# A one-core layer with 32 experts: order of the routing weights, of the second expert's copies, of two experts' loads and of the last squares

## The reference, cut to what matters

```python
lg = (t @ p['w_router_group'] + p['b_router_group']).astype(F32)
pg = jax.nn.softmax(lg, axis=-1)
grp = jnp.argmax(lg, axis=-1)
...
top_p, top_i = lax.top_k(pe, TOP_K)
wts = p_grp * top_p / jnp.sum(top_p, axis=-1, keepdims=True)
...
for e in range(N_EXPERTS):
    z = jax.nn.silu(t @ p['w1'][e]) * (t @ p['w3'][e])
    y = y + gates[:, e:e + 1] * (z @ p['w2'][e])
...
x = x + g2 * hier_moe(h, p)
y_sample = rmsnorm(xs, g_final)
```

## Time and profile before

| | |
|---|---|
| median of 3 runs | 979.88 us (977.21 to 982.35) |
| profiled execution | 981.13 us |
| its span, first to last instruction | 979.3 us |
| busy, PE / DVE / POOL / ACT | 91% / 61% / 32% / 28% of the span |
| chain of work that ended last, by engine | PE 59%, DMA 19%, DVE 15%, ACT 4% |
| granted clock of PE, mean | 0.974 |

### The profile page before, as it was taken

One profiled execution on the slowest core, in us unless ns is written; L12 is line 12 of the kernel. 1 busy time (PEld: TensorE's weight loads), 2 busy tenths in 40 slices (PEclk: granted clock), 3 DMA queues, 4 the chain that ended last, 5 costly groups with the idle time before them and its releaser, 6 DMA issues.

```text
span 979.3 us, 12372 instructions
## 1 busy us (share of the span) xinstructions
PE 890.1 (91%) x4480; PEld 552.6 (56%) x4480; DVE 594.1 (61%) x957; ACT 278.0 (28%) x468; POOL 310.2 (32%) x232
## 2 busy tenths in 40 slices
PE   3898898999899999999899999999989888889994
PEld 1688796989899999845333333333333333333331
DVE  2589696859211552235447677677767666657667
ACT  4374636463143432011211111112111111212112
POOL 0046262636255545222222133133222131313100
PEclk9799899999999999999789999999999999999998
DMA  9962272646464347445689999999999999999981
GB/s 343 358 226 94 78 254 97 224 142 237 172 215 165 137 152 262 177 205 212 252 309 417 407 415 424 415 419 413 396 392 414 398 404 394 410 400 410 408 355 66
DMA packets 59849, 285.69 MB, mean 292 GB/s; under 512 B 6655, under 2 KB 11039, under 8 KB 47252
## 3 DMA queue, kind: packets, MB, share of 16 engines
q1 hardware_dynamic: 56196, 278.63, 73.5%
q0 software_dynamic: 2480, 3.11, 1.1%
q10 hardware_dynamic: 1120, 3.24, 0.9%
HBM read 286.80 MB, written 3.19 MB: 296 GB/s over the span
## 4 chain that ended last, share of the span: by engine, by line
PE 59%; DMA 19%; DVE 15%; ACT 4%; issue 2%; SPq 1%; DVEq 0%; POOL 0%; ACTq 0%
PE bank L1084 12%; PE bank L1097 8%; PE bank L878 7%; PE bank L879 7%; PE bank L880 7%; DMA ring<-in_w 7%; DMA slot<-in_w 6%; PE bank L934 4%; PE bank L1085 4%; DMA gate_w<-in_w 3%; DVE xcy L1672 3%; DVE xcy L2038 3%; DMA ring<-in_w_ada 2%; PE bank L1061 2%; PE bank L814 1%
## 5 line engine op out<-in xcount | busy, mean ns | idle before, releaser
L475 POOL TENSOR_TENSOR subs<-ring,subs 128x1024 fp32r<-128x1024 f32 x69 | 177.6, 2581 | 222.2 <-ACT subs L1225 222.2
L878 PE MATMUL bank<-h_hl,subs 128*128 128x384 f32 x488 | 167.8, 344 | 12.0 <-ACT lru L1304 4.6
L879 PE MATMUL bank<-h_hl,subs 128*128 128x384 f32 x488 | 165.7, 340 | 0.0
L880 PE MATMUL bank<-h_hl,subs 128*128 128x384 f32 x488 | 165.6, 339 | 0.0
L2013 DVE TENSOR_TENSOR lru<-bank,cp 128x512 f32<-128x512 f32 x186 | 116.3, 678 | 55.0 <-PE bank L1061 55.0
L1084 PE MATMUL bank<-ring,x_T 128*64 128x512 f32 x256 | 119.6, 611 | 8.2 <-DMA ring<-in_w 3.3
L1085 PE MATMUL bank<-ring,x_T 128*64 128x512 f32 x256 | 118.1, 604 | 0.0
L2022 DVE TENSOR_TENSOR hg<-hg,lru 128x512 f32<-128x512 f32 x186 | 116.6, 679 | 0.0
L878 PEld LDWEIGHTS bank<-h_hl,subs 128*128 128x128 f32 x488 | 92.9, 190 | 19.3 <-issue 9.6
L665 POOL COPY idx<-lists 64x1 uint32 (+1 forms) x31 | 5.5, 177 | 294.8 <-PE bank L1039 294.8
L1084 PE MATMUL bank<-slot,x_T 128*64 128x512 f32 x192 | 88.6, 605 | 8.5 <-DMA slot<-in_w 6.0
(11 more groups left out here) (245 smaller groups left out, 1506.0 us busy)
## 6 DMA issues: line engine op xcount, KB each, us to landing
ring<-in_w SPq DMA_DIRECT2D x46, 2048.0 KB, 26.6
slot<-in_w SPq DMA_DIRECT2D x36, 2048.0 KB, 27.1
ring<-in_w_in SPq DMA_DIRECT2D x14, 2048.0 KB, 8.0
ring<-in_w_ada SPq DMA_DIRECT2D x12, 2048.0 KB, 9.1
gate_w<-in_w SPq DMA_DIRECT2D x12, 2048.0 KB, 26.9
ring<-in_w_rnn_out SPq DMA_DIRECT2D x2, 2048.0 KB, 8.4
ring<-in_w_conv_out SPq DMA_DIRECT2D x2, 2048.0 KB, 8.1
ring<-in_w_o SPq DMA_DIRECT2D x2, 2048.0 KB, 8.2
```

The lines of the kernel that those rows point to most:

```text
L475: eng.tensor_tensor(pair[:, 1], src, pair[:, 0].bitcast(F32), ALU.subtract).then_inc(done, 1)
L878: eng.matmul(ps[:, 0:T], pair[:, 1, k, :], x[:, 0, k, :], start=(k == 0), stop=False)
L879: eng.matmul(ps[:, 0:T], pair[:, 0, k, :], x[:, 1, k, :], start=False, stop=False)
L880: mm = eng.matmul(ps[:, 0:T], pair[:, 0, k, :], x[:, 0, k, :], start=False, stop=(k == KD - 1))
```

## The change

Four places are written in another order.

1. DVE works out the three tiles' weights ahead of the copies of the list, and ACT takes the exponentials ahead of the copies of expert 0's rows. POOL copies expert 0's weight column directly behind its token column, ahead of the gather for expert 1; the waits for the stored rows move behind it.
2. For expert 0, ACT and DVE copy the transposed rows of expert 1 ahead of the parts of y.
3. Expert 30 is loaded in the pieces in which expert 31 is: its w1 now waits for y of expert 27 too. Its `hidden` waits in two steps.
4. At the end ACT squares tile t + 1 ahead of the root of tile t.

```diff
@@ -400,5 +400,5 @@
         gated = sem("spread_times_gain")
         added = sem("spread_added")
-        half_landed = [sem(f"last_half_landed{w}") for w in range(2)]
+        half_landed = [[sem(f"half_landed{x}{w}") for w in range(2)] for x in range(2)]
         last_y_ready = sem("last_y_times_gain")
         step_v = sem("vector_step")
@@ -615,17 +615,23 @@
                 for s in range(LAP):
                     load_expert(i * LAP + s, s)
-            for s in range(LAP - 1):
+            for s in range(LAP - 2):
                 load_expert(NE - LAP + s, s)
-            multiplied_in(NE - 4)
-            multiplied_out(NE - 4)
-            part = KD * CW // 2
-            for w, src in enumerate((w1_v, w3_v)):
-                eng.dma_start(moe_slots[moe_slot(LAP - 1, w)][:, 0:part], src[NE - 1][:, 0:part])\
-                    .then_inc(half_landed[w], 16)
-            for w, src in enumerate((w1_v, w3_v)):
-                n = moe_slot(LAP - 1, w)
-                eng.dma_start(moe_slots[n][:, part:], src[NE - 1][:, part:]).then_inc(moe_landed[n], 16)
-            multiplied_in(NE - 3)
-            load(NE - 1, LAP - 1, 2)
+
+            def load_in_halves(e, s):
+
+                part = KD * CW // 2
+                multiplied_in(e - 3)
+                multiplied_out(e - 3)
+                for w, src in enumerate((w1_v, w3_v)):
+                    eng.dma_start(moe_slots[moe_slot(s, w)][:, 0:part], src[e][:, 0:part])\
+                        .then_inc(half_landed[LAP - 1 - s][w], 16)
+                for w, src in enumerate((w1_v, w3_v)):
+                    n = moe_slot(s, w)
+                    eng.dma_start(moe_slots[n][:, part:], src[e][:, part:]).then_inc(moe_landed[n], 16)
+                multiplied_in(e - 2)
+                load(e, s, 2)
+
+            for s in (LAP - 2, LAP - 1):
+                load_in_halves(NE - LAP + s, s)
             eng.wait_ge(flag_ready, 1)
             most = eng.value_load(flag[0:1, 0:1], min_val=0, max_val=T)
@@ -734,13 +740,13 @@
             wait_read(eng, ("list",))
             eng.wait_ge(flag_ready, 1)
+            token_column(0, 0)
+            eng.wait_ge(slot_weights, 1)
+            weight_column(0, 0)
             for t in range(TT):
                 eng.wait_ge(h2_out[t], 16)
-            token_column(0, 0)
             eng.wait_ge(xg_used, 1)
             gather(1, 1)
             token_column(1, 1)
-            eng.wait_ge(slot_weights, 1)
-            for e in range(2):
-                weight_column(e, e)
+            weight_column(1, 1)
             for e in range(2, 4):
                 eng.wait_ge(xg_used, e - 1)
@@ -1068,7 +1074,8 @@
                 if not first:
                     eng.wait_ge(z_ready, e)
-                if last:
-                    eng.wait_ge(half_landed[0], 16)
-                    eng.wait_ge(half_landed[1], 16)
+                halves = isinstance(i, int) and i == NE // LAP - 1 and s >= LAP - 2
+                if halves:
+                    eng.wait_ge(half_landed[LAP - 1 - s][0], 16)
+                    eng.wait_ge(half_landed[LAP - 1 - s][1], 16)
                 else:
                     wait_weights(eng, i, s, 0)
@@ -1079,5 +1086,5 @@
                     if k == 3:
                         between()
-                    if last and k == KD // 2:
+                    if halves and k == KD // 2:
                         wait_weights(eng, i, s, 0)
                         wait_weights(eng, i, s, 1)
@@ -1480,4 +1487,6 @@
             root(2)
             store(2)
+            for t in range(TT):
+                top_exps(t)
             ps, _ = tile(("x0",))
             eng.wait_ge(h2_out[1], 16)
@@ -1486,6 +1495,4 @@
             eng.activation(x_T[:, 0:4, :], bank[FIRST_T[0]][:, :].rearrange("p (m t) -> p m t", m=4)[:, :, 0:HALF], ACT.Copy)\
                 .then_inc(xT_a, 1)
-            for t in range(TT):
-                top_exps(t)

             def rows_copy(e):
@@ -1519,8 +1526,8 @@
                     rows_copy(e + 1)
                 zT_copy(e)
+                if first:
+                    rows_copy(1)
                 if not last:
                     y_hi(i, s, e)
-                if first:
-                    rows_copy(1)

             for s in range(LAP):
@@ -1554,4 +1561,10 @@
                 eng.wait_ge(o_added, TT)

+            def last_root(t):
+
+                eng.wait_ge(mean_ready, TT + t + 2)
+                eng.activation(stat[:, 2, 2, t:t + 1], stat[:, 2, 1, t:t + 1], ACT.Sqrt)\
+                    .then_inc(rms_ready, 1)
+
             eng.activation(stat[:, 1, 2, 0:1], stat[:, 1, 1, 0:1], ACT.Sqrt)
             for t in range(TT):
@@ -1561,7 +1574,7 @@
                 eng.activation(o_junk, x_rows[:, t, :], ACT.Square, accum_out=stat[:, 2, 0, t:t + 1])\
                     .then_inc(ssq_ready, 1)
-                eng.wait_ge(mean_ready, TT + t + 2)
-                eng.activation(stat[:, 2, 2, t:t + 1], stat[:, 2, 1, t:t + 1], ACT.Sqrt)\
-                    .then_inc(rms_ready, 1)
+                if t:
+                    last_root(t - 1)
+            last_root(TT - 1)
             eng.wait_ge(state_out, 16)

@@ -1978,4 +1991,6 @@
             wait_read(eng, ("count",))
             eng.tensor_copy(flag[:, :], cmax[:, :]).then_inc(flag_ready, 1)
+            for t in range(TT):
+                weights(t)
             ps, free = tile(("list",))
             eng.tensor_scalar(slot_token[:, :], ps[:, 0:NE], float(UNUSED), None, ALU.add)
@@ -2061,6 +2076,4 @@
                                                   in1=last_gain[rows, :], op0=ALU.mult, op1=ALU.add))

-            for t in range(TT):
-                weights(t)
             eng.wait_ge(weights_done, 1)
             eng.tensor_copy(slot_weight[:, :], bank[7][0:CAP, 0:NE]).then_inc(slot_weights, 1)
```

## The result

The changed kernel takes 981.96 us (median of 20 runs, 978.56 to 984.02) where the kernel before, run beside it, takes 978.73 (20 runs). The ratio is 1.0024, with an interval of 1.0015 to 1.0032: slower by some 2 to 3 us. The forecast was 2.25 us faster. The change lies within 0.5%, yet its sign was wrong, and a version with one of its parts taken back (the first experiment) is 0.45% faster than the kernel before. The profiled execution of after took 983.96 us (span 982.1).

What follows compares the result with a forecast made beforehand. The weight stream bounds the middle; only its restart at expert 1, the stall before expert 30 and the tail can move the end. 0 + 0.65 - 1.8 - 1.1 = -2.25 us gave a median of 977.6 us, range 975.0 to 981.8.

Steps and rivals of the forecast that it cites:

- What bounds the kernel: Middle of the expert stage: lasts as long as its weight transfers; the stream restarts when expert 1's hidden products finish.
- Weights on DVE and ACT: Before expert 0: earlier weights and exponentials gain nothing, since PE's order holds the sums behind expert 0's products; taken as 0.
- the cover of 0.2 us: On ACT before expert 0: the moved exponentials end at 471.2, the copy they now precede started at 471.38.
- Halves: Before expert 30: loading in halves removes PE's 1.80 us slot wait; gain 1.8 us, between 0 and 2.3.
- Squares: Final norm: the second square fills ACT's 1.30 us of idleness, so the first norm starts earlier; gain 1.1 us.
- The copies alone: Expert 1's start: with x_T copies first, products follow the transposes by 0.55 us, 1.03 us earlier if the gather is timely.
- POOL's gather beside the loads: Expert 1's gather: issued about 485.75, lands in 8.1 us; PE waits 1.6 us, products start 0.65 us later, copies included.
- rival C: Expert 1's products: PE's clock drops after the idle time, costing 5.6 us more; +3.35 in all, 983.2 us; chance 0.10.
- Rival A: Expert 1's gather: not late, as its packets pass between the weights'; -3.9 us in all, 976.0 us; chance 0.22.
- Rival B: Experts 30 and 31: halves do nothing, the wait only moves to second halves or expert 31; 979.4 us; chance 0.18.

Runs made afterwards that it cites:

- the first experiment: The changed kernel with GpSimd's old order back: expert 1's gather goes out first again, ahead of the wait for slot_weight; 974.27 us, 0.9955 of the kernel before.
- PE kept busy: The changed kernel plus six constant products on PE ahead of expert 1's transposes, during the wait for the gather; 980.02 us, 1.0003 of the kernel before.
- The held loads: The changed kernel with SyncE also waiting for expert 1's gather to land before issuing loads from w2 of expert 2 on; 979.33 us, 1.0003 of the kernel before.
- weights alone: The kernel before with only the new order of weights on DVE and exponentials on ACT, GpSimd's order old; 979.65 us, 0.9995 of the kernel before.
- squares alone: The kernel before with only the squares put ahead of the roots at the end; 978.16 us, 0.9992 of the kernel before.
- halves alone: The kernel before with only expert 30 loaded in halves, as expert 31 is; 977.45 us, 0.9982 of the kernel before.

## Why the prediction was wrong

**What bounds the kernel: right.** Expert 1's products set the restart of the stream, and the time followed them: gather first 500.66 and 974.3, PE kept busy 505.53 and 980.0, after 508.14 and 982.0. The held loads are the case in which the stream's other end moved.

**Weights on DVE and ACT: right** in time, nothing gained or lost; in the traces expert 0's transposes wait 1.07 us for ACT's copy where they waited 0.89 for DVE's, so the cover of 0.2 us was about 0.2 short. **Halves: right**, -1.8 forecast and measured. **Squares: right in the trace**, -1.1 forecast, 1.09 in the profile; in time -0.8, not told apart from either.

**The copies alone: right** (1.03 forecast, 1.0 in the trace).

**POOL's gather beside the loads: the step that failed.** The forecast saw that the gather would go out behind slot_weight, meet the loads and land late, and put a wait of 1.6 us and a shift of +0.65 on it. Measured: a wait of 4.09 us. Against the very execution that the forecast was worked from, the length from the loads to the products' end grew by 23.70 - 20.93 = 2.77 us where 0.65 was forecast: 0.9 more of the landing, and products of 10.87 us where that execution had 504.63 - 495.00 = 9.63. Against an execution of the old code at full clock it grew by 23.70 - 17.67 = 6.0. Three things were missing.

First, when PE is ready. The 492.31 of the earlier trace rows lies 8.61 us behind the loads' issue, but that execution ran expert 0's y at a granted clock of 0.58 (the loads and the window before, then the transposes of weights alone):

```profile
483.70 0.80 SPq L573 DMA_DIRECT2D ring<-in_w  x2
...
488.00:492.00 4.00, 4.00 (x14) 1.04 (x10) 0.00 (x0) 0.00 (x0) 0.00 (x0) 0.58 1.02 433
```

```profile
492.24 1.11 PE L1039 MATMUL bank<-ident,xcy 80*128 80x80 f32 x8
```

At full clock (weights alone, 492.24 against 485.32) it is 6.9, so PE arrives 1.7 us earlier and waits 1.7 longer. In reading I took a start that the clock had delayed for the time at which PE is always ready. That shift is hidden when before and after are compared in that one execution, and comes out in the median, if most executions of before are like weights alone and squares alone: to a wait, an engine that arrives earlier is no gain.

Second, the landing: 8.8 us where I took 8.1, and an issue 2.26 us behind the loads where I took 2.05. That is another 0.9; with the first the wait is 1.6 + 1.7 + 0.9 = 4.2, against the measured 4.09.

Third, rival C. I gave it 0.10 and held it apart from the forecast, with the argument that the idle time is about as short as before. Idle time became 4.09 + 0.56 us, and the products ran at the low clock from their start to past 502; about 2.7 us in the trace, 1.9 in time. Since C's cause is the very wait of the forecast, it should have been a term of the sum whose size grows with the wait, not an outcome beside it.

With these, the sum is 23.70 - 17.67 = +6.0 us at expert 1, less 1.8 and 1.1: +3.1 against an execution of before at full clock there. Measured: +3.2 between the medians, +2.3 by the ratio.

**Rival A: its packets do pass, but late and slowly; its price was about right.** Beside the loads the rows landed in 8.8 and 8.9 us, without them in 2.9 and 3.2, although the packets of the two queues take turns, 105 against 118. That agrees with the rule that the Trainium skill gives ("DMA: Bandwidth & Descriptors", Queues, rings and completion order: each DMA engine takes packets from its queues in turn), and shows that the rule is no promise that a small gather is quick beside 2 MB loads. The same page's fit (Anatomy of one DMA: 2.0 us plus bytes over 436 GB/s) gives an estimate of 2.6 us for 64 rows of 4 KB, near the landings without loads only. With the gather in time, A's -3.9 compares with the first experiment's -5.2 between medians and -4.4 by the ratio. **Rival B** is refuted by the halves alone.

**What stays open:** why the gather's packets begin over 4.2 us behind the issue beside the loads and some 2 us behind it without them; and how often an execution of before meets the low clock between 488 and 492. Of the four profiles with its code there, before and halves alone did, squares and weights alone did not. Over all ten profiles the four with a low clock in that stretch are the four whose clock was back at 0.90 or more between 478 and 480, in expert 0's products; the other six had 0.50 to 0.82 there. All five kernels with the new order of the weights are among the six. Whether that order brings it about was not tested. In after's profile expert 31's y also ran partly at the low clock (0.73 and 0.84 between 962 and 970), which neither was forecast nor tested: from the products' end to the last instruction it took 2.2 us more than with the gather first (982.1 - 508.14 against 972.4 - 500.66). It may be this execution's alone, which lies 2.0 us above after's median.

## What to carry to other kernels

A small gather on the critical path should be issued while the queues are idle: before it is put behind a wait, look at what else that wait's event releases, here 4 MB of loads in the same microsecond. A wait is priced from when its engine is ready in an undisturbed execution, and its price includes the clock at which the engine goes on behind it and the transfers that its work releases. A change of several parts can hide one that harms: taking the parts one by one showed 4 to 5 us to be had where the whole lost 2 to 3.

## What the runs showed of the hardware

A gather of 64 rows landed in 2.9 to 3.2 us in idle or nearly idle queues, whether issued at 481 or at 486.7, and in 8.8 to 8.9 us beside the two loads of 2 MB, whose packets of 16 KB it had to take turns with, one for one. Throwaway products during a wait of 4 us on TensorE kept the granted clock at 1.00, where it fell to 0.53 without them, and brought 1.9 us of time although the rows came no earlier. And the granted clock over one and the same code differed from one execution to the next: 0.58 and 1.00 between 488 and 492 us in two kernels that are alike there (before and squares alone), 3.3 us apart in the length above; the slow one had left the low clock earlier in the products ahead of it, 1.00 against 0.52 between 478 and 480.
